# An attention and short-convolution block on eight cores: squares of x0 ahead of the sines, loads of the prologue in a chain, some squares on VectorE

## The reference

```python
h = rmsnorm(x, norm_g)
z = h @ w_in            # latents q_a (512), kv_a (256), rope key k_pe (64), gates, conv inputs
q = rmsnorm(q_a) @ w_uq ; kv = rmsnorm(kv_a) @ w_ukv        # 16 heads of 128 + 64
q, k = rmsnorm per head, then rope(cos, sin of positions) on the last 64
attn = softmax(q k^T / sqrt(192)) v                          # all 2048 keys
y_attn = (attn * silu(gate_a)) @ w_branch_attn
y_conv = (B * conv3(C * xin) * silu(gate_c)) @ w_branch_conv
x = x + (sigmoid(m_a) * y_attn + sigmoid(m_c) * y_conv) @ w_out
x = x + sigmoid(rmsnorm(x) @ w_ple_gate) * (p @ w_ple_proj)
```

## Time and profile before

| | |
|---|---|
| profiled execution, time | 1676.92 us |
| its span (slowest core, core 4) | 1675.4 us |
| spans of the 8 cores | 1666.6 to 1675.4 us |
| PE busy | 1563.7 us (93% of the span) |
| DVE busy | 775.1 us (46%) |
| ACT busy | 741.5 us (44%) |
| share of PE in the chain that ended last | 85% |
| PE busy, 0 to 60 us | 24.35 us |
| PE busy, 60 to 75 us | 7.12 us |
| PE busy, 90 to 160 us | 63.69 us |

### The profile page before, as it was taken

How to read it: one execution, slowest core, us unless ns; L and a number is a source line. 1 busy time by engine, 2 the same in 40 slices (tenths; PEclk the granted TensorE clock), 3 DMA queues, 4 the chain that set the end, 5 groups by cost and what they waited for, 6 DMA issues and landing times.

```text
span 1675.4 us, 22557 instructions; the slowest of 8 cores (1666.6 to 1675.4 us)
## 1 busy us (share of the span) xinstructions
PE 1563.7 (93%) x7511; PEld 735.2 (44%) x7660; DVE 775.1 (46%) x999; ACT 741.5 (44%) x1234; POOL 94.0 (6%) x181
## 2 busy tenths in 40 slices
PE   3698898999999989999999999999999999999998
PEld 0143454444444534444445444444444444444443
DVE  6226466757667666766776211111111111243554
ACT  3344476777777768777785311000010101243211
POOL 0000000000000000000000110000100110000000
PEclk9799999999999999999999999999999999999999
DMA  9750221202021111211111684345444544974511
GB/s 258 192 130 13 45 39 20 39 15 40 18 38 32 24 22 32 39 19 20 26 26 26 107 140 75 63 70 88 72 73 76 89 69 85 211 172 81 119 70 70
DMA packets 37889, 119.02 MB, mean 71 GB/s; under 512 B 3984, under 2 KB 4112, under 8 KB 36240
## 3 DMA queue, kind: packets, MB, share of 16 engines
q0 software_dynamic: 25488, 82.85, 29.5%
q1 hardware_dynamic: 12288, 34.72, 6.4%
HBM read 192.00 MB, written 8.39 MB: 120 GB/s over the span
## 4 chain that ended last, share of the span: by engine, by line
PE 85%; ACT 4%; issue 4%; DVE 3%; DMA 2%; SPq 0%; ACTq 0%; POOL 0%; DVEq 0%; POOLq 0%
PE ps_s L775 6%; PE ps_o L833 6%; PE ps_s L773 6%; PE ps_s L968 4%; PE ps_s L930 3%; PE ps_s L900 3%; PE ps_s L891 3%; PE ps_s L894 3%; PE ps_s L872 3%; PE ps_o L894 3%; PE ps_a L900 3%; PE ps_o L891 3%; PE ps_s L416 2%; PE ps_b L897 2%; PE ps_o L872 2%
## 5 line engine op out<-in xcount | busy, mean ns | idle before, releaser
L780 ACT ACTIVATE arena<-ps_s,arena 128x512 bf16<-128x512 f32 x512 | 324.0, 685 | 64.8 <-PE ps_s L775 56.6
L820 DVE TENSOR_TENSOR arena<-arena 128x1024 f32<-128x1024 f32 x224 | 273.2, 1220 | 21.1 <-ACT arena L780 16.0
L775 PE MATMUL ps_s<-arena 128*128 128x512 bf16 x507 | 194.0, 383 | 0.8 <-issue 0.2
L773 PE MATMUL ps_s<-arena 128*128 128x512 bf16 x501 | 191.2, 382 | 2.8 <-ACT arena L780 2.2
L833 PE MATMUL ps_o<-arena 128*128 128x512 bf16 x478 | 145.8, 381 | 1.6
L773 PEld LDWEIGHTS ps_s<-arena 128*128 128x128 bf16 x512 | 50.3, 98 | 64.9 <-issue 5.7
L775 PEld LDWEIGHTS ps_s<-arena 128*128 128x128 bf16 x512 | 50.4, 98 | 60.7 <-issue 1.6
L903 ACT ACTIVATE arena<-ps_o 128x512 f32<-128x512 f32 x16 | 9.6, 597 | 129.6 <-PE ps_o L891 121.5
L833 PEld LDWEIGHTS ps_o<-arena 128*128 128x128 bf16 x512 | 49.1, 98 | 36.8 <-issue 1.6
L905 DVE SCALAR_TENSOR_TENSOR arena<-arena,ps_s 128x512 f32<-128x512 f32 x16 | 11.0, 689 | 115.7 <-PE ps_s L897 108.5
L903 ACT ACTIVATE arena<-ps_s 128x512 f32<-128x512 f32 x16 | 9.6, 597 | 124.2 <-PE ps_s L891 124.2
(11 more groups left out here) (276 smaller groups left out, 2540.3 us busy)
## 6 DMA issues: line engine op xcount, KB each, us to landing
arena<-w_dense POOLq DMA_DIRECT2D x48, 512.0 KB, 5.3
arena<-w_merge POOLq DMA_DIRECT2D x48, 512.0 KB, 5.9
arena<-x_fm SPq DMA_DIRECT2D x20, 1024.0 KB, 26.0
arena<-w_pg POOLq DMA_DIRECT2D x16, 576.0 KB, 6.0
arena<-w_out POOLq DMA_DIRECT2D x16, 512.0 KB, 7.3
out<-arena SPq DMA_DIRECT2D x32, 256.0 KB, 2.0
arena<-x_fm SPq DMA_DIRECT2D x8, 512.0 KB, 13.7
arena<-w_q POOLq DMA_DIRECT2D x16, 256.0 KB, 3.7
```

The source lines that it names most:

```text
L773: P.op("pe", lambda h, bk=bk, qs=qs: h.matmul(bk.ap, lhsT=Kb.ap[:, kt * 128:(kt + 1) * 128], rhs=Qa.ap[:, qs], start=True, stop=False), re ...
L775: P.op("pe", lambda h, bk=bk, qs=qs: h.matmul(bk.ap, lhsT=KrT.ap[:, kt * 128:(kt + 1) * 128], rhs=Qb.ap[:, qs], start=False, stop=True), r ...
L780: P.op("act", lambda h, sb=sb, qb=qb: h.activation(out=pt.ap[:, qb * 512:(qb + 1) * 512], in_=sb.ap, func=AF.Exp, scale=so.ap[:, kt:kt + 1 ...
L820: P.op("dve", lambda h, pt=pt, ac=ac: h.tensor_tensor(out=ac.ap, in0=ac.ap, in1=pt.ap, op=ALU.add), reads=R(ac, *pt.rl), writes=R(ac))
```

## The change

The order of the loads changes: x0 as a whole, WlK, then x1, whose issue on SP waits until the third of the four parts of WlK has landed, then WlQ, and x2 waits until the third part of WlQ has landed. The second half of the positions (`posrow[1]`) and `cmb` are issued on SP behind x1 (before: among and behind x0). The Sin for TABa stands behind the Exp of x0's norm; the DVE part of TABb stands behind `A_b(0)`, and its Sin between `e1_sq(0)` and the squares of x1. The odd squares (j = 1, 3, 5, 7) of x1 and x2 go to DVE. The squares of x2 are recorded 4 matmuls earlier.

```diff
-        def load_x(blk, n=4, qs=None):
+        def load_x(blk, n=4, deps=()):
...
-                             b.slots[q], writes=b.rl[w // 2 * q:w // 2 * (q + 1)])
+                             b.slots[q], writes=b.rl[w // 2 * q:w // 2 * (q + 1)], deps=deps)
...
-        load_x(0, 8, range(3))
+        load_x(0, 8)
+        lk = [ld("pool", WlK.ap[:, 4 * q:4 * q + 4, :], w_latk_d[:, 4 * q:4 * q + 4, :], WlK.rl[q], P.slot(f"wk{q}"), deps=half[0:1]) for q in range(4)]
+        load_x(1, deps=lk[2:3])
+        lq = [ld("pool", WlQ.ap[:, 4 * q:4 * q + 4, :], w_latq_d[:, 4 * q:4 * q + 4, :], WlQ.rl[q], P.slot(f"wl{q}"), deps=half[1:2]) for q in range(4)]
         ld("sp", posrow[1].ap, pos_d[:, 1024:2048], posrow[1], P.slot("pos1"))
-        load_x(0, 8, range(3, 8))
...
         ld("sp", cmb.ap, cmb_d, cmb, s_c)
-        load_x(1)
...
         def A_sq(blk, j):
             b, sq = xb[blk % 2], sqx[j % 2]
+            xa = b.ap[:, 2 * j:2 * j + 2, :]
+            if j % 2 and blk in (1, 2):
+                P.op("dve", lambda h: h.tensor_tensor(out=sq.ap, in0=xa, in1=xa, op=ALU.mult), reads=R(b.rl[j]), writes=R(sq))
+            else:
+                P.op("act", lambda h: h.activation(out=sq.ap, in_=xa, func=AF.Square), reads=R(b.rl[j]), writes=R(sq))
...
-        table(TABa, posrow[0])()
-        sin_b = table(TABb, posrow[1])
+        sin_a = table(TABa, posrow[0])
         P.op("act", lambda h: h.activation(out=rq.ap[:, 0:1], in_=col(COL_EPS), func=AF.Ln), reads=R(cols), writes=R(rq))
         for j in range(8):
             A_sq(0, j)
         A_rs(0)
+        sin_a()
         A_b(0)
-        load_x(2)
-        sin_b()
+        load_x(2, deps=lq[2:3])
+        sin_b = table(TABb, posrow[1])
         run(lat(0, WlK, 3, kbanks[0]), {})
         e1_sq(0)
+        sin_b()
         for j in range(3):
             A_sq(1, j)
...
-        run([...], ins((6, lambda: e2_mm(0)), *[(16 + 5 * j, lambda j=j: A_sq(2, j)) for j in range(8)]))
+        run([...], ins((6, lambda: e2_mm(0)), *[(12 + 5 * j, lambda j=j: A_sq(2, j)) for j in range(8)]))
```

More of the change, by code:

```diff
@@ L325, in load_x @@
             last = None
-            for q in (range(n) if qs is None else qs):
+            for q in range(n):
                 last = P.dma("sp", lambda h, q=q: h.dma_start(out=b.ap[:, w * q:w * q + w, :], in_=x_d[blk][:, w * q:w * q + w, :]),
-                             b.slots[q], writes=b.rl[w // 2 * q:w // 2 * (q + 1)])
+                             b.slots[q], writes=b.rl[w // 2 * q:w // 2 * (q + 1)], deps=deps)
                 if q == n // 2:
@@ L333, in build_nc @@
         half = []
-        load_x(0, 8, range(3))
+        load_x(0, 8)
+        lk = [ld("pool", WlK.ap[:, 4 * q:4 * q + 4, :], w_latk_d[:, 4 * q:4 * q + 4, :], WlK.rl[q], P.slot(f"wk{q}"), deps=half[0:1]) for q in range(4)]
+        load_x(1, deps=lk[2:3])
+        lq = [ld("pool", WlQ.ap[:, 4 * q:4 * q + 4, :], w_latq_d[:, 4 * q:4 * q + 4, :], WlQ.rl[q], P.slot(f"wl{q}"), deps=half[1:2]) for q in range(4)]
         ld("sp", posrow[1].ap, pos_d[:, 1024:2048], posrow[1], P.slot("pos1"))
-        load_x(0, 8, range(3, 8))
[L337 to L340, removed]
         ld("sp", cmb.ap, cmb_d, cmb, s_c)
-        load_x(1)
-        for q in range(4):
-            ld("pool", WlQ.ap[:, 4 * q:4 * q + 4, :], w_latq_d[:, 4 * q:4 * q + 4, :], WlQ.rl[q], P.slot(f"wl{q}"), deps=half[0:1])
         P.op("dve", lambda h: h.memset(ones.ap, 1.0), writes=R(ones))
@@ L382, in A_sq @@
             b, sq = xb[blk % 2], sqx[j % 2]
-            P.op("act", lambda h: h.activation(out=sq.ap, in_=b.ap[:, 2 * j:2 * j + 2, :], func=AF.Square), reads=R(b.rl[j]), writes=R(sq))
+            xa = b.ap[:, 2 * j:2 * j + 2, :]
[3 more added lines that the diff above has]
+                P.op("act", lambda h: h.activation(out=sq.ap, in_=xa, func=AF.Square), reads=R(b.rl[j]), writes=R(sq))
             for i in range(2):
@@ L511, in build_nc @@
         m4 = lat(1, WlQ, 4, qbanks[1])
-        run([m4[4 * kc + m] for kc in range(16) for m in range(3)] + m4[3::4], ins((6, lambda: e2_mm(0)), *[(16 + 5 * j, lambda j=j: A_sq(2, j)) for j in range(8)]))
+        run([m4[4 * kc + m] for kc in range(16) for m in range(3)] + m4[3::4], ins((6, lambda: e2_mm(0)), *[(12 + 5 * j, lambda j=j: A_sq(2, j)) for j in range(8)]))
         A_rs(2)
```

## The result

The changed kernel takes 1686.3 us (two executions, 1685.77 and 1686.88), the kernel before 1677.0 (four, 1676.92 to 1677.48); the ratio is 1.0057 with a 95% interval of 1.004 to 1.0073, so it is slower by 0.57%. Predicted were 1686.7 us, range 1680.5 to 1692.

A forecast was written before the change was run, and what follows sets the result against it. PE is busy for 93% of the span, so the prediction asked how far the prologue's end, `A_b(1)`, moves. 1676.93 us plus 6.8 (later `A_b(1)`) plus 2.95 (squares of x2) gave 1686.7 us, range 1680.5 to 1692.

The forecast's parts named there:

- Step 1: Squares of x0 run as chunks land; `A_b(0)` begins at 27.1, 4.6 us earlier, not yet a gain of the path.
- Step 2: WlK's third part at about 30.3, block 0's matmuls end at 38 to 41: 13 us gained if nothing else late.
- Step 3: Second positions, issued behind x1 on SP, land at 49 (bounds 46 and 53), and TABb and its Sin wait for them.
- first rival: Positions overtake x1, landing at 37 or so; `A_b(1)` at 70.4, 4.3 us earlier, kernel not slower; chance 0.08.
- Step 4: From the positions' landing to `A_b(1)`: x1's first square 4.7 us later, chain 2.0 longer, `A_b(1)` at 81.5, 6.8 later.
- Step 5: Squares of x2: PE waits 1.41 us for ACT and 2.1 for DVE, and comes 2.95 us later to the stream's end.
- Rival 3: Waits at x2's squares and longer PE idleness from 41 to 61 cost extra slow matmuls: 1690.5 us; chance 0.15.
- Rival 2: Late positions hold, but DVE's squares of x1 and x2 cost nothing: 1681.6 us; chance 0.12.

The follow-up runs named there:

- e6: Kernel before with only x1's issue made to wait for the third part of WlK: 1669.56 us, ratio 0.996 to the kernel before.
- e2: Changed kernel with all eight squares of x1 on ACT again: 1685.05 us, ratio 1.0055 to the kernel before.
- e7: Kernel before with only the odd squares of x1 and x2 on DVE and x2's recorded from matmul 12 on: 1682.2 us, ratio 1.0035.
- e3: Changed kernel with the squares of x2 all on ACT and recorded from matmul 16 on again: 1682.92 us, ratio 1.0036 to the kernel before.
- e1: Changed kernel with the second half of the positions issued right behind x0, ahead of x1: 1675.68 us, ratio 0.9992 to the kernel before.
- e5: Changed kernel with second positions right behind x0, Sin of TABb behind Exp of x1's norm plus one-column Ln, all squares on ACT, x2's from matmul 16: 1663.76 us.

## Why the prediction was right, point by point

**Step 1** gave `A_b(0)` at 27.1; it began at 25.16. x0 landed sooner than a mere 1.7 us for the positions: chunk 4 at 16.97 instead of 20.63. The start of `A_b(0)` was not on the path, so this miss cost nothing. But chunk 4 is, as it releases WlK: 16.97 instead of the 18.9 predicted, 3.7 us sooner than before where 1.7 were counted. What makes up the other 2 us was not looked into. 1.3 us of it were left at WlK, 1.1 at the positions and 0.5 at `A_b(1)`.

**Step 2**: WlK's third part predicted at 30.3, landed at 29.0, and the matmuls of block 0 ended before 39, as said. This gain exists, and in e6 most of it reaches the end. The pace of q0 in this step, 0.169 MB per us, is not what its row gives: 2.43 MB in 14 us is 0.174, and WlK's 1.57 MB take 9.0 us instead of 9.3. That is too little to matter here.

**Step 3** is the term that decided. Predicted landing of the positions 49, first instruction of TABb at 47.98. Single loads of the changed kernel, issued on SP at 31.24 (last part of x1), 31.99 and 32.47: KB, us to landing:

```profile
arena<-x_fm SPq DMA_DIRECT2D x1, 1024.0 KB, 14.3
...
arena<-pos_row SPq DMA_DIRECT2D x1, 512.0 KB, 15.9
...
arena<-cmb SPq DMA_DIRECT2D x1, 64.0 KB, 16.2
```

They landed at 45.5, 47.9 and 48.7, in order. The first rival, that the positions overtake x1, is refuted on this queue. The Trainium skill's rule on it ("DMA: Bandwidth & Descriptors", Queues, rings and completion order) says that completion is not in order within an issuing engine, and its case is a later DMA on one of the 16 DMA engines behind an earlier one on all 16. The prediction carried it over to two loads that both fill 128 partitions, which that case does not cover; here the measurement decides against overtaking. The pace I used, q1 alone, was right too, in 31 to 45 us (packets, MB, share):

```profile
q1 hardware_dynamic: 613, 4.30, 97.7%
```

4.30 MB in 14 us is 0.307 MB per us, against 0.308 in the earlier trace rows.

**Step 4**: the end of TABb to `A_b(1)`: predicted 22.8, measured 58.01 to 80.96, 22.95. From the first square 21.9 against 21.7. e2 and e7 show its cause, the square behind the scalings: j = 3 at 68.84, directly behind them.

**Step 5**: waits of 1.41 and 1.94 against 1.41 and 2.1, where one of 0.55 was. e3 takes them down to 0.55; its stretch from `A_b(1)` to `A_b(3)` is 2.2 us shorter and its time 3.4 less.

**Where it was right by some luck.** I worked from core 4 alone. Its positions landed late (47.98; cores 3, 5 and 7 began TABb at 43.5 to 44.1). The mean of `A_b(1)` moved by 5.65, not 6.8, that of `A_b(3)` by 8.4, and the mean span by 7.7; the time moved by 9.3 (1686.3 against 1677.0). The difference of 1.6 us is in the slowest core: the changed kernel's core 4 had a mean granted clock of 0.978 against 0.983. I did not find what decides which core that is.

Two misses on core 4 cancel. From `A_b(1)` to `A_b(3)` it lost 2.35 us and not 2.95 (65.89 before, 68.24 after). The waits do grow by 2.8, but PE came back to full clock sooner: its first 48 matmuls of block 1 took 12.38 us instead of 12.99. Behind `A_b(3)`, where the two kernels have the same instructions, core 4 then took 1.3 us more (1536.1 against 1534.8), while the mean over the cores took 0.7 less. No step foresaw that. Between the cores of one execution this last part differs by 6 us (1530.0 to 1536.2 in the changed kernel).

Rival 3, the clock, finds nothing to stand on in this pair of profiled executions. At the squares of x2 (105 to 125 us) the granted clock of the changed kernel is 1.00 on all eight cores, so the two waits did not bring it down. The first 48 or 49 matmuls of block 1 took 12.6 us in the mean, against 12.8 before, so the longer idleness of PE did not keep it at half for longer. Rival 2, free DVE squares, is refuted by e3 and e7.

## What to carry to other kernels

Here a load of 0.5 MB moved behind one of 4 MB on the same queue landed behind all of it, and all that stood in program order behind its reader paid. Look up, for each load that is moved, the first instruction that waits for it, and all that this engine and the next do in the meantime. An instruction for a result that is needed only much later (here a Sin, whose table is first read at 147.91 us on core 4 of the changed kernel) belongs in a gap of its engine, with its table loads. Before a series of short operations is shared between two engines, look for what stands ahead of each part: here a piece of the other engine came behind work that waited for the first engine's, or behind TABb. No run here shows sharing to gain.

## What the runs showed of the hardware

Two things I had not expected. The first: the granted clock of PE behind `A_b(1)` differs between cores of one execution that do the same work. Two cores of e1, three stretches of 5 us each from the first matmul of block 1 on (PE, PEld, DVE, ACT, POOL busy with counts, then the granted clock, DMA share, GB/s):

```profile
core 2 of [0, 1, 2, 3, 4, 5, 6, 7], span 1669.0 us
...
69.00:74.00 5.00, 4.78 (x12) 1.74 (x13) 5.00 (x9) 0.00 (x0) 0.00 (x0) 0.50 0.99 410
74.00:79.00 5.00, 5.00 (x24) 2.19 (x23) 5.00 (x8) 0.00 (x0) 0.00 (x0) 0.96 1.04 351
79.00:84.00 5.00, 5.00 (x23) 2.16 (x21) 0.26 (x2) 1.57 (x3) 0.00 (x0) 0.89 0.96 292
```

```profile
core 7 of [0, 1, 2, 3, 4, 5, 6, 7], span 1672.7 us
...
70.50:75.50 5.00, 4.74 (x14) 1.84 (x15) 5.00 (x9) 0.00 (x0) 0.00 (x0) 0.61 0.81 297
75.50:80.50 5.00, 5.00 (x25) 2.23 (x23) 5.00 (x8) 0.00 (x0) 0.00 (x0) 1.00 0.96 265
80.50:85.50 5.00, 5.00 (x24) 2.24 (x23) 0.80 (x2) 1.58 (x3) 0.00 (x0) 1.00 0.99 311
```

Core 2 comes through its first 49 matmuls in 13.54 us, core 7 in 12.54, and core 2 then falls to a mean of 0.89 once more, though PE is busy all through on both. Two different things are mixed in this. How long PE stays at half its clock differs from core to core (these matmuls took 12.1 to 13.2 us in the changed kernel). The second fall is shared by a die: in 82 to 84 us the granted clock was 0.81 on each of cores 0 to 3 and 1.00 on each of cores 4 to 7, and by 90 us it was back at 1.00 on all. In the profiled executions of the kernel before, of the changed kernel and of e5 no core fell again in the 20 us behind `A_b(1)`. The mean of the first 48 or 49 matmuls was 13.1 us in e1 and 12.6 in the changed kernel, so this explains at most the 0.9 us that e1 lost between `A_b(1)` and `A_b(3)`, not the whole of its miss. Nor does it pick the slowest core: core 2 ends at 1669.0 us, before core 7 at 1672.7. What sets either I can't say; no run here was made for it.

The second: where TABb runs behind `A_b(0)`, DVE stands 0.52 to 0.53 us between its first and second instruction (48.67 to 49.20 in the rows above, the same in e1 and e5), while directly behind TABa, in the kernel before, it stood for none. The profile names nothing that it waited for but the first instruction. It is small and left open; with it the end of TABb came 10.0 us after its start instead of 9.6.
